# Attention core of a fused two-block kernel: one group of transposes moved ahead of the last score products

## The chip, the cores and the metric

The program runs on one NeuronCore of a Trainium2 chip, in float32 throughout. The metric is the time of one execution on the device in microseconds (us). The core has TensorE (PE in the profile, with its weight loads shown apart as PEld), VectorE (DVE), ScalarE (ACT), GpSimd (POOL) and SyncE (SP, which only issues DMAs here). Each engine works through its own list of instructions in order and waits for the others by semaphores.

## What is computed

Two transformer-like blocks run one after the other in one program. The change touches one part of the first: the attention of 1024 tokens, in 16 heads of 64 values each (8 grouped-query heads on 2 key and value heads, then 8 latent heads with 64 + 32 key dimensions), over 1280 keys, of which 256 come from a context.

```python
def block_attention(q, k, v, scale):
    ...
    def one_block(qi):
        s = jnp.einsum("bqhgd,bkhd->bhgqk", _f32(qi), kf) * scale
        p = jax.nn.softmax(s, axis=-1)
        return jnp.einsum("bhgqk,bkhe->bqhge", p, vf)
...
        o_a = block_attention(q_a, k_a, v_a, GQA_HEAD_DIM ** -0.5)
        o_m = block_attention(q_m, k_m, v_m, (MLA_NOPE_DIM + MLA_ROPE_DIM) ** -0.5)
        o = jnp.concatenate([o_a, o_m], axis=-1)
        return (o * jax.nn.silu(gate)) @ w_out
```

## The kernel before

The attention core is a loop of 64 **stages**. Stage s treats 128 tokens (s // 8) and one pair of heads (p = s % 8, the heads called e = 0 and 1). Pairs 0 to 3 are grouped-query heads, pairs 4 to 7 latent heads. A stage has these steps:

- **Scores** (`scores_pe`, L793 to L819), PE. Each head has its own three PSUM banks, `attn_aux` for e = 0 and `attn_far` for e = 1, for 1280 scores, filled in segments of 512, 512 and 256 keys. A product of L808 uses 64 rows of the array, so the two heads' products lie side by side in it. Latent heads add products over 32 rows for the rotated part: L816 for the first 1024 keys, L819 for the last 256. A float32 product appears as two matmul instructions, each `x1` in the rows. The last segment's products count `scored`.
- **Maximum** (`maximum` in `core_dve`), DVE: for each head one `reduce_max` over its 1280 scores (L915) and a small negation (L917), which counts `negated`.
- **Softmax weights** (`soften` in `core_act`), ACT: for each head one exponential over 1280 scores with the sum accumulated (L896), which counts `exped`. The sum is read out by a short second instruction on the same line.
- **Turn** (`turn_group_pe`, L822 to L839), PE: the weights are transposed in five **groups** j = 0 to 4 of four 128x128 transposes, each group into one of two banks of `attn_dense`: groups 0, 2 and 3 into bank 0, groups 1 and 4 into bank 1. A transpose uses the whole 128x128 array.
- **Copies** out of those banks: groups 0, 1 and 3 by ACT (L885), groups 2 and 4 by DVE (L922). A group waits for the copy that empties its bank (`copied[0]`, `copied[1]`).
- **Weigh** (`weigh_pe`, L843 to L852), PE: 20 products of values and turned weights, 40 instructions on 64 columns of the array, into bank 1; DVE keeps the result (`keep`, L928, counts `stored`). It waits for all copies of its stage, and for this stage's copy 1 and so for bank 1.

The loop is software-pipelined by hand in `core_pe`. In iteration s PE waits for the exponentials of stage s, then does: all scores of stage s + 1, groups 0, 1 and 2 of stage s, the weighing of stage s - 1, groups 3 and 4 of stage s. ACT does copy 0, copy 1, the two exponentials of stage s + 1, copy 3. DVE does a reciprocal (L943), the two maxima of stage s + 1, copy 2, the keep of stage s - 1, copy 4, and once per eight stages a multiplication (L934). So group 3 waits for copy 2, which stands on DVE behind both maxima of the next stage; group 4 waits for the keep, which stands behind copy 2. SP issues DMAs only for the sums, once per eight stages.

After stage 63 comes the rest of the kernel, beginning with the gate projections (L122), which wait for the last keep.

Of the kernel before, what the change touches and what calls it, by code (L numbers as in the profile page):

```python
# [15 lines left out]
L = 1024  # L16
LT = L // P
C = 256
N = L + C
# [5 lines left out]
ROPE = 32  # L25
# [38 lines left out]
def segments(cols):  # L64

    return [(a, min(a + BANK, cols)) for a in range(0, cols, BANK)]
# [88 lines left out]
STAGES = 8 * LT  # L155
# [569 lines left out]
def values_pe(pe, Y, t):  # L725

    if t == 0:
        pe.wait_ge(Y.aux_read, len(Y.use))
    elif t == 2:
        pe.wait_ge(Y.vm_read, 1)  # L730
    elif t == 3:
        pe.wait_ge(Y.vm_read, 2)
    elif t == 4:
        pe.wait_ge(Y.va_read, 2)
    elif EARLY <= t < EARLY + 2:
        pe.wait_ge(Y.dense.emptied[t - EARLY], Y.dense.at["u7"] + 1)
    elif t >= EARLY:
        pe.wait_ge(Y.vm_read, t - 1)
    pe.matmul(values_bank(Y, t), Y.ckv[:, t * P:(t + 1) * P], Y.wv[:], start=True, stop=True).then_inc(Y.vm_filled, 1)
# [47 lines left out]
def stage(s):  # L787

    t, p = divmod(s, 8)
    return slice(t * P, (t + 1) * P), p  # L790


def scores_pe(pe, Y, s):  # L793

    tokens, p = stage(s)
    if s:
        pe.wait_ge(Y.exped, 2 * s)
    else:
        pe.wait_ge(Y.km_read, 4)
        pe.wait_ge(Y.vm_read, EARLY)  # L800
        pe.wait_ge(Y.va_read, len(OWN_GROUPS))
        pe.wait_ge(Y.roped, len(ROPES))
        Y.dense.done(pe, "u3")
    for lo, hi in segments(N):
        for e in range(2):
            rows = slice(64 * e, 64 * e + 64)
            keys = Y.ka[rows, lo:hi] if p < 4 else Y.km[rows, p - 4, lo:hi]
            mm = pe.matmul(Y.scores[e][:, lo:hi], Y.Q[rows, p, tokens], keys, start=True, stop=(p < 4))  # L808
            if p < 4 and hi == N:
                mm.then_inc(Y.scored, 1)  # L810
    if p >= 4:
        for e in range(2):
            for n, (lo, hi) in enumerate(segments(L)):
                first = 64 * e + ROPE * n
                rows = slice(first, first + ROPE)
                pe.matmul(Y.scores[e][:, lo:hi], Y.Q[rows, p + 4, tokens], Y.kpe[rows, lo:hi], start=False, stop=True)  # L816
        for e in range(2):
            rows = slice(64 * e, 64 * e + ROPE)
            pe.matmul(Y.scores[e][:, L:N], Y.Q[rows, p + 4, tokens], Y.kpe[rows, L:N], start=False, stop=True).then_inc(Y.scored, 1)  # L819


def turn_group_pe(pe, Y, s, j):  # L822

    bank = Y.banks[j % 2] if j < 3 else Y.banks[(j + 1) % 2]
    if s == 0 and j < 2:
        pe.wait_ge(Y.vm_read, NT)
    if s or j >= 2:
        if j in (0, 2, 3):
            pe.wait_ge(Y.copied[0], 3 * s + (0, 0, 1, 2)[j])
        elif j == 1:  # L830
            pe.wait_ge(Y.copied[1], 2 * s)
        else:
            pe.wait_ge(Y.copied[1], 2 * s + 1)
            if s:
                pe.wait_ge(Y.stored, s)
    for e in range(2):
        for kk in range(2):
            n, k = 2 * e + kk, 2 * j + kk
            tr = pe.transpose(bank[:, n * P:(n + 1) * P], Y.probs[:, s % 2, e, k * P:(k + 1) * P], Y.ident)  # L839
    tr.then_inc(Y.turned_up, 1)  # L840


def weigh_pe(pe, Y, s):  # L843

    tokens, p = stage(s)
    bank = Y.banks[1]
    pe.wait_ge(Y.copied[1], 2 * (s + 1) + (1 if s + 1 < STAGES else 0))
    pe.wait_ge(Y.copied[0], 3 * (s + 1))
    for k in range(NT):
        for e in range(2):  # L850
            v = Y.va[:, k, 64 * e:64 * e + 64] if p < 4 else Y.vm[:, k, HD * (2 * (p - 4) + e):HD * (2 * (p - 4) + e + 1)]
            mm = pe.matmul(bank[64 * e:64 * e + 64, 0:P], v, Y.turned[:, s % 2, 4 * (k // 2) + 2 * e + k % 2], start=(k == 0),  # L852
                           stop=(k == NT - 1))
    mm.then_inc(Y.weighed, 1)


def core_pe(pe, Y):
    scores_pe(pe, Y, 0)
    for t in range(EARLY, NT):
        values_pe(pe, Y, t)  # L860
    for s in range(STAGES):
        pe.wait_ge(Y.exped, 2 * s + 2)
        if s + 1 < STAGES:
            scores_pe(pe, Y, s + 1)
        for j in range(3):
            turn_group_pe(pe, Y, s, j)
        if s:
            weigh_pe(pe, Y, s - 1)
        for j in (3, 4):
            turn_group_pe(pe, Y, s, j)  # L870
    weigh_pe(pe, Y, STAGES - 1)
# [269 lines left out]
def attention_layer(nc, arena, A, x_out, mod, one_plus, K):  # L1141
    with Phase(nc, "attn") as ph:
        Y = Attention(nc, ph, arena, A, mod, one_plus, K)
        with ph.block() as block:
            @block.sync
            def _(sp):
                attention_sp(sp, Y)
                store_halves(sp, Y, x_out)

            @block.tensor  # L1150
            def _(pe):
                front_pe(pe, Y)
                core_pe(pe, Y)
                back_pe(pe, Y)

            @block.scalar
            def _(act):
                front_act(act, Y, A["x"], A["ctx"])
                core_act(act, Y)
                back_act(act, Y)  # L1160

            @block.vector
            def _(dve):
                front_dve(dve, Y)
                core_dve(dve, Y)
                back_dve(dve, Y)
# [2780 lines left out]
```

## Time and profile before

| | us |
|---|---|
| runs of the kernel (3) | 4828.37, 4829.55, 4832.45; median 4829.55 |
| profiled execution: device time | 4826.16 |
| profiled execution: span, first to last instruction | 4824.4 |
| PE busy | 4628.4 (96%) |
| DVE busy | 2090.0 (43%) |
| ACT busy | 1008.9 (21%) |
| the attention core in the span | from 297.8 to 853.3 |

The busy shares are means over the whole kernel. The attention core is about a ninth of it and repeats itself: between the first and last few stages, an iteration that scores a grouped-query pair looks like every other such iteration, and one that scores a latent pair likewise. What the change does can be read from one iteration of each kind, start by start: the profile gives each instruction's start and duration, and for an idle engine who released it. Ends of matmuls are modelled, so that consecutive ones overlap in the rows; for PE, the distance of starts is what counts. The granted clock was 1.00 in the core except for its first 13 us.

### The profile page before, as it was taken

To read this page: it belongs to the slowest core of one execution; us is meant where nothing else is said; L and a number is where in the kernel's file an instruction comes from. 1 tells how busy PE (TensorE), PEld (TensorE's weight loads), DVE (VectorE), ACT (ScalarE), POOL (GpSimd) and SP (SyncE) were. 2 spreads that over 40 slices of the span, in tenths; PEclk is the share of its full clock that TensorE was granted. 3 is DMA by queue.
4 is the path that set the end of the run, shared out by engine and by line. 5 is a ranking of instruction groups with operands and counts; after the bars stand their busy time and mean duration, and the time that the engine had idled before them with its cause. 6 is when DMAs were issued, how large, how long until landed. Compare 5 with 4: busy or idle time off the path is not lost.

```text
span 4824.4 us, 39417 instructions
## 1 busy us (share of the span) xinstructions
PE 4628.4 (96%) x16488; PEld 2291.1 (47%) x16488; DVE 2090.0 (43%) x2485; ACT 1008.9 (21%) x1349; POOL 3.9 (0%) x7
## 2 busy tenths in 40 slices
PE   7999999999999999999999999999999999999998
PEld 3456666443444444554555554444444444444443
DVE  3555555134333466644344433513643354333412
ACT  3145555111111100002333222322310010000000
POOL 0000000000000000000000000000000000000000
PEclk9999999998999999999999999999999999999999
DMA  6100000222231522221111011012231131111211
GB/s 247 71 27 10 10 10 6 105 78 88 81 105 69 197 101 104 100 97 57 40 35 36 32 35 42 33 44 74 72 107 39 40 109 48 44 44 44 76 44 55
DMA packets 106812, 320.27 MB, mean 66 GB/s; under 512 B 26085, under 2 KB 44261, under 8 KB 99082
## 3 DMA queue, kind: packets, MB, share of 16 engines
q1 hardware_dynamic: 89708, 306.22, 17.9%
q10 hardware_dynamic: 16928, 11.54, 0.7%
q8 instruction: 131, 2.15, 0.2%
q14 instruction: 45, 0.37, 0.0%
HBM read 257.36 MB, written 60.36 MB: 66 GB/s over the span
## 4 chain that ended last, share of the span: by engine, by line
PE 67%; DVE 8%; issue 1%; DMA 1%; ACT 1%; DVEq 0%; SPq 0%; ACTq 0%
PE late_dense L122 31%; PE late_four L3281 10%; PE late_two L3281 5%; PE late_four L3510 3%; PE late_four L1403 3%; PE late_four L2341 2%; PE late_four L1592 2%; PE late_dense L3510 1%; PE late_two L1680 1%; PE late_two L1672 1%; PE late_four L1420 1%; PE late_four L1415 1%; PE late_two L3510 1%; PE late_two L1609 1%; DVE arena L2577 1%
## 5 line engine op out<-in xcount | busy, mean ns | idle before, releaser
L122 PE MATMUL late_dense<-arena 128*128 128x512 f32 x4008 | 1778.0, 601 | 18.5 <-ACT arena L135 7.6
L122 PEld LDWEIGHTS late_dense<-arena 128*128 128x128 f32 x4008 | 765.1, 193 | 960.5 <-issue 951.5
L3281 PE MATMUL late_four<-arena 128*128 128x512 f32 x1160 | 506.5, 594 | 5.9 <-DVE arena L3111 5.9
L135 ACT ACTIVATE arena<-late_dense 128x512 f32<-128x512 f32 x198 | 118.0, 596 | 1162.2 <-PE late_dense L122 1140.6
L3281 PEld LDWEIGHTS late_four<-arena 128*128 128x128 f32 x1160 | 221.1, 191 | 284.7 <-issue 274.9
L122 PE MATMUL attn_dense<-arena 128*128 128x512 f32 x640 | 281.3, 597 | 4.2 <-ACT arena L637 2.1
L3281 PE MATMUL late_two<-arena 128*128 128x512 f32 x576 | 253.4, 592 | 0.0
L3329 DVE TENSOR_TENSOR arena<-late_four,arena 128x512 f32<-128x512 f32 x145 | 98.7, 690 | 300.5 <-PE late_four L3281 296.1
L839 PE MATMUL attn_dense<-matrices,arena 128*128 128x128 f32 x1280 | 187.6, 282 | 18.2 <-ACT arena L885 16.1
L122 PEld LDWEIGHTS attn_dense<-arena 128*128 128x128 f32 x640 | 121.1, 191 | 158.5 <-issue 153.8
L1403 PE MATMUL late_four<-arena 128*128 128x512 f32 x384 | 171.6, 600 | 7.8 <-DMA arena<-in_hy_tables 3.9
L3281 PEld LDWEIGHTS late_two<-arena 128*128 128x128 f32 x576 | 109.4, 190 | 137.8 <-issue 135.8
L839 PEld LDWEIGHTS attn_dense<-matrices,arena 128*128 128x128 f32 x1280 | 135.4, 141 | 72.2 <-issue 32.1
L885 ACT ACTIVATE arena<-attn_dense 128x512 f32<-128x512 f32 x192 | 107.8, 596 | 242.4 <-PE attn_dense L839 234.4
L915 DVE TENSOR_REDUCE arena<-attn_aux 128x1 f32<-128x1280 f32 x64 | 95.5, 1491 | 145.2 <-PE attn_far L819 90.2
L808 PE MATMUL attn_aux<-arena 64*128 64x512 f32 (+1 forms) x384 | 156.0, 540 | 1.6 <-ACT arena L770 0.8
L808 PE MATMUL attn_far<-arena 64*128 64x512 f32 (+1 forms) x384 | 156.1, 540 | 0.0
L852 PE MATMUL attn_dense<-arena 128*64 128x128 f32 x2560 | 153.9, 275 | 0.8 <-DVE arena L922 0.8
L852 PEld LDWEIGHTS attn_dense<-arena 128*64 128x64 f32 x2560 | 138.4, 137 | 11.6 <-ACT arena L885 10.6
L3510 PE MATMUL late_four<-arena 128*128 128x512 f32 x320 | 139.0, 592 | 0.0
L2341 PE MATMUL late_four<-arena 128*128 128x64 f32 (+3 forms) x1024 | 97.7, 283 | 26.5 <-DVE arena L2489 14.3
L1403 PEld LDWEIGHTS late_four<-arena 128*128 128x128 f32 x384 | 72.5, 191 | 100.7 <-issue 93.1
(384 smaller groups left out, 4703.0 us busy)
## 6 DMA issues: line engine op xcount, KB each, us to landing
arena<-in_ada_w SPq DMA_DIRECT2D x12, 2048.0 KB, 8.5
arena<-in_w_ffn_in SPq DMA_DIRECT2D x44, 512.0 KB, 4.0
arena<-in_hy_tables SPq DMA_DIRECT2D x16, 1280.0 KB, 6.1
arena<-in_hy_w_in SPq DMA_DIRECT2D x32, 512.0 KB, 3.3
spectrum<-arena SPq DMA_DIRECT2D x8, 2048.0 KB, 8.8
arena<-spectrum SPq DMA_DIRECT2D x8, 2048.0 KB, 12.7
arena<-in_w_gates SPq DMA_DIRECT2D x32, 512.0 KB, 3.3
spill<-arena SPq DMA_DIRECT2D x26, 512.0 KB, 4.4
```

The lines of the kernel that those rows point to most:

```text
L122: mm = pe.matmul(self.ps[:, n % SEG], self.wbuf[:, slot, k], job.rhs[:, k, cols], start=(job.first and k == 0), stop=(job.last and k == kt ...
L135: act.activation(job.out[:, cols], self.ps[:, n % SEG], job.func, scale=job.scale, bias=job.bias).then_inc(self.emptied[n % SEG], 1)
L808: mm = pe.matmul(Y.scores[e][:, lo:hi], Y.Q[rows, p, tokens], keys, start=True, stop=(p < 4))
L839: tr = pe.transpose(bank[:, n * P:(n + 1) * P], Y.probs[:, s % 2, e, k * P:(k + 1) * P], Y.ident)
L852: mm = pe.matmul(bank[64 * e:64 * e + 64, 0:P], v, Y.turned[:, s % 2, 4 * (k // 2) + 2 * e + k % 2], start=(k == 0), stop=(k == NT - 1))
L885: act.activation(dst, src, ACT.Copy).then_inc(sem, 1)
L1403: mm = pe.matmul(Y.group[:, 2 * a + part], Y.table[:, r, part, k], rhs[:, 2 * r + k], start=(k == 0), stop=(k == 1))
L1592: mm = pe.matmul(group[:, 2 * (q % 2) + way], Y.hid[:, q * P:(q + 1) * P], Y.mix[:, way, cols], start=True, stop=True)
L2341: mm = pe.matmul(ps[:, (u + h) % 2, queries], left[t.rows[h], at], right[t.rows[h], queries], start=True, stop=True)
L3281: mm = pe.matmul(product_bank(M, name, i), left[:, k], right[:, k], start=(k == 0), stop=(k == 3))
L3329: dve.tensor_tensor(out, product_bank(M, product, i), other, ALU.add).then_inc(M.summed_up, 1)
L3510: mm = pe.matmul(bank, left[:, k], right[:, k], start=(first and k == 0), stop=(last and k == count - 1), skip_group_check=True)
```

## The change

The score products of the last 256 keys leave `scores_pe` for a function of their own, `last_scores_pe`. In iteration s PE now does: the scores of stage s + 1 but for that last piece, group 0 of stage s, the last piece of the scores, groups 1 and 2, and then the weighing and groups 3 and 4 as before. For a grouped-query pair the last piece is L808's segment of 256 keys (2 products, 4 instructions); for a latent pair it is L819's (also 2 products, 4 instructions), while L808's three segments stay ahead. Every instruction stays, with its operands and its semaphores; nothing changes on ACT, DVE, POOL or SP.

```diff
-    for lo, hi in segments(N):
-        for e in range(2):
-            rows = slice(64 * e, 64 * e + 64)
-            keys = Y.ka[rows, lo:hi] if p < 4 else Y.km[rows, p - 4, lo:hi]
-            mm = pe.matmul(Y.scores[e][:, lo:hi], Y.Q[rows, p, tokens], keys, start=True, stop=(p < 4))
-            if p < 4 and hi == N:
-                mm.then_inc(Y.scored, 1)
+    for lo, hi in segments(N)[0:2 if p < 4 else 3]:
+        head_scores_pe(pe, Y, s, lo, hi)
     if p >= 4:
...
-        for e in range(2):
-            rows = slice(64 * e, 64 * e + ROPE)
-            pe.matmul(Y.scores[e][:, L:N], Y.Q[rows, p + 4, tokens], Y.kpe[rows, L:N], start=False, stop=True).then_inc(Y.scored, 1)
+
+
+def head_scores_pe(pe, Y, s, lo, hi):
+
+    tokens, p = stage(s)
+    for e in range(2):
+        rows = slice(64 * e, 64 * e + 64)
+        keys = Y.ka[rows, lo:hi] if p < 4 else Y.km[rows, p - 4, lo:hi]
+        mm = pe.matmul(Y.scores[e][:, lo:hi], Y.Q[rows, p, tokens], keys, start=True, stop=(p < 4))
+        if p < 4 and hi == N:
+            mm.then_inc(Y.scored, 1)
+
+
+def last_scores_pe(pe, Y, s):
+
+    tokens, p = stage(s)
+    if p < 4:
+        head_scores_pe(pe, Y, s, L, N)
+        return
+    for e in range(2):
+        rows = slice(64 * e, 64 * e + ROPE)
+        pe.matmul(Y.scores[e][:, L:N], Y.Q[rows, p + 4, tokens], Y.kpe[rows, L:N], start=False, stop=True).then_inc(Y.scored, 1)
...
 def core_pe(pe, Y):
     scores_pe(pe, Y, 0)
+    last_scores_pe(pe, Y, 0)
...
         if s + 1 < STAGES:
             scores_pe(pe, Y, s + 1)
-        for j in range(3):
+        turn_group_pe(pe, Y, s, 0)
+        if s + 1 < STAGES:
+            last_scores_pe(pe, Y, s + 1)
+        for j in (1, 2):
             turn_group_pe(pe, Y, s, j)
```

## Rows read from the trace of the kernel before

**Rows 1.** The page's first line: the span of the profiled execution.

```profile
span 4824.4 us, 39417 instructions
```

**Rows 2.** Stretches: us, busy of PE, PEld, DVE, ACT, POOL, PEclk, DMA, GB/s.

```profile
307.90:311.20 3.30, 3.29 (x8) 1.62 (x10) 0.07 (x1) 0.35 (x1) 0.00 (x0) 0.50 0.00 0
311.20:319.00 7.80, 5.54 (x38) 3.41 (x34) 4.56 (x7) 4.41 (x7) 0.00 (x0) 1.00 0.00 0
450.00:850.00 400.00, 387.62 (x3696) 269.58 (x3692) 233.47 (x383) 211.99 (x330) 0.00 (x0) 1.00 0.05 9
```

**Rows 3.** Timeline, PE, one iteration scoring a grouped-query pair: start us, us, instruction.

```profile
580.37 0.69 PE L808 MATMUL attn_aux<-arena 64*128 64x512 f32 x1
580.90 0.59 PE L808 MATMUL attn_aux<-arena 64*128 64x512 f32 x1
...
582.19 0.38 PE L808 MATMUL attn_aux<-arena 64*128 64x256 f32 x1
...
582.41 0.38 PE L808 MATMUL attn_aux<-arena 64*128 64x256 f32 x1
...
582.72 1.09 PE L839 MATMUL attn_dense<-matrices,arena 128*128 128x128 f32 x8
584.06 0.66 PE L839 MATMUL attn_dense<-matrices,arena 128*128 128x128 f32 x4 [0.25 <-ACT arena L885]
584.65 2.40 PE L852 MATMUL attn_dense<-arena 128*64 128x128 f32 x40
```

**Rows 4.** Timeline, PE, in narrow windows around its changes of work there.

```profile
582.89 0.49 PE L839 MATMUL attn_dense<-matrices,arena 128*128 128x128 f32 x3
...
584.45 0.27 PE L839 MATMUL attn_dense<-matrices,arena 128*128 128x128 f32 x1
...
586.78 0.28 PE L852 MATMUL attn_dense<-arena 128*64 128x128 f32 x2
586.99 0.33 PE L839 MATMUL attn_dense<-matrices,arena 128*128 128x128 f32 x1
...
587.90 0.27 PE L839 MATMUL attn_dense<-matrices,arena 128*128 128x128 f32 x1
588.10 0.69 PE L808 MATMUL attn_aux<-arena 64*128 64x512 f32 x1
```

**Rows 5.** Timeline, DVE, same iteration.

```profile
582.82 1.49 DVE L915 TENSOR_REDUCE arena<-attn_aux 128x1 f32<-128x1280 f32 x1 [1.58 <-PE attn_far L808]
...
586.00 0.68 DVE L922 COPY arena<-attn_dense 128x512 f32<-128x512 f32 x1
587.11 0.29 DVE L928 COPY arena<-attn_dense 128x128 f32<-128x128 f32 x1 [0.42 <-PE attn_dense L852]
```

**Rows 6.** Timeline, ACT, same iteration: copies 0 and 1, and the second exponential's read-out.

```profile
583.41 0.60 ACT L885 ACTIVATE arena<-attn_dense 128x512 f32<-128x512 f32 x1 [2.86 <-PE attn_dense L839]
583.91 0.59 ACT L885 ACTIVATE arena<-attn_dense 128x512 f32<-128x512 f32 x1
...
587.35 0.19 ACT L896 ACTIVATION_READ_ACCUMULATOR arena<-attn_far,arena 128x1 f32 x1
```

**Rows 7.** Timeline, PE and DVE, one iteration scoring a latent pair, and the next's start.

```profile
631.21 0.69 PE L808 MATMUL attn_aux<-arena 64*128 64x512 f32 x1
...
635.15 1.49 DVE L915 TENSOR_REDUCE arena<-attn_aux 128x1 f32<-128x1280 f32 x1 [3.07 <-PE attn_far L819]
...
640.43 0.69 PE L808 MATMUL attn_aux<-arena 64*128 64x512 f32 x1
```

**Rows 8.** Timeline, the first iteration's group 3, and the turn of iterations 62 and 63.

```profile
315.90 1.09 PE L839 MATMUL attn_dense<-matrices,arena 128*128 128x128 f32 x8 [2.01 <-DVE arena L922]
...
843.06 0.19 ACT L896 ACTIVATION_READ_ACCUMULATOR arena<-attn_far,arena 128x1 f32 x1
843.40 0.60 ACT L885 ACTIVATE arena<-attn_dense 128x512 f32<-128x512 f32 x1
```

**Rows 9.** Waits from 319 to 840 us: total us, times, longest.

```profile
PE attn_dense L839 <- ACT arena L885: 15.6, 62, 0.3
```

## Prediction

> **What bounds the kernel now.** I read first where the change acts: the attention core, 297.8 to 853.3 us of a span of 4824.4 us [rows 1]. The stretches show PE busy for 387.62 of 400 us there, DVE and ACT for little more than half, clock 1.00 [rows 2]. Then I took the timeline of one iteration, engine by engine. From one first score product to the next it lasts 588.10 - 580.37 = 7.73 us where a grouped-query pair is scored [rows 3, 4], and 640.43 - 631.21 = 9.22 us where a latent pair is [rows 7]. PE sets this length, with one real gap: the eight transposes of groups 0 and 1 last start at 582.72 + 1.09 - 0.27 = 583.54, and group 2 starts at 584.06, 0.05 us after copy 0 ends (583.41 + 0.60) [rows 3, 4, 6]. That is 0.41 us more than the usual step of 0.11 from transpose to transpose ((0.49 - 0.27)/2) [rows 4], and the waits list it 62 times [rows 9]. It is the gap that the move closes: with score products between groups 0 and 1, copy 0 is over before group 2 is due.
>
> The second thing to read is how late the other chain runs, from the last score product through DVE: both maxima, copy 2, group 3. From the start of the first maximum to that of copy 2 are 586.00 - 582.82 = 3.18 us, copy 2 takes 0.68 [rows 5]; I add 0.05 for the handover to PE, as at copy 0. Were group 3 to start there, then groups 3 and 4 take 0.82 from first to last start (as groups 0 and 1: 1.09 - 0.27) and the next scores start 0.20 later (587.90 to 588.10) [rows 3, 4]. Sum: 3.18 + 0.68 + 0.05 + 0.82 + 0.20 = 4.93 us from maximum to next iteration. Now the maximum starts at 2.45 us into the iteration (582.82 - 580.37), or at 3.94 in a latent one (635.15 - 631.21) [rows 3, 5, 7]. 2.45 + 4.93 = 7.38 against 7.73, and 3.94 + 4.93 = 8.87 against 9.22: this chain has a **slack of 0.35 us** in either kind.
>
> **The change, part by part.** Nothing is removed or added; three things move.
>
> *Group 0 earlier.* Its copy is off ACT's hands before copy 1 is wanted. Gains the 0.41 us at group 2 and no more; what comes next is worked out below.
>
> *The last score products later.* The maximum waits for them. They now stand behind four transposes: 4 x 0.11 = 0.44 us [rows 4]. No row of before has score products between transposes, so the two additional changes of work are priced by the rows of such changes elsewhere. Into transposes: from the last products at 582.41 to 582.72 are 0.31 us, where two products of 256 keys are 582.41 - 582.19 = 0.22 apart, so 0.09 extra, and the first transpose takes 0.17 (582.72 to 582.89) instead of 0.11, another 0.06: 0.15 [rows 3, 4]. Into products: 587.90 to 588.10 is 0.20 instead of 0.11, and the first product takes 0.53 (580.37 to 580.90) instead of 0.43 (a third of 580.90 to 582.19): 0.19 [rows 3, 4]. Together 0.34 us an iteration. The bounds: nothing at all from below (a transpose after a transpose pays nothing, though it waits on a semaphore), and twice this from above; changes from and to the weighing cost the same 0.09 (584.45 to 584.65, and 586.78 to 586.99, against 0.11) [rows 3, 4], so I take 0.34.
>
> The Trainium skill, "TensorEngine Tiling (Array Packing)", section Key Properties, says that a change of tiling mode drains TensorE. The rows agree: 64-row products, full transposes and 64-column weighing each cost some 0.09 us to enter. A reader who counted instructions alone would find no cost in this move; by that page each interleaving costs two drains, which speaks against the change, and without them my sum would be that of the cheap case below.
>
> *The maximum, and all behind it.* It starts 0.44 + 0.34 = **0.78 us later**; the slack is 0.35. Queued behind it on DVE are copy 2 and the keep, and on ACT the exponentials and copy 3; PE's group 3 waits for copy 2. In the grouped-query iteration: maximum at 3.23, copy 2 ends at 3.23 + 3.18 + 0.68 = 7.09, group 3 at 7.14, next scores at 3.23 + 4.93 = 8.16 us. Not later than that: the weighing waits for copy 1, which starts now 583.91 - 583.54 = 0.37 after the last transpose of group 1 (0.31 when ACT is free: 583.41 less group 0's last start, 582.89 + 0.22), so at 3.17 + 0.34 + 0.31 = 3.82, ends at 4.41, and the weighing starts at 4.46 and would let group 3 go at 4.46 + (586.99 - 584.65 = 2.34) = 6.80, before 7.14 [rows 3, 4, 6]. The keep ends at 7.09 + 0.29 = 7.38, before group 4 is due at 7.14 + 0.17 + 3 x 0.11 = 7.64 [rows 5]. The exponentials end 587.35 + 0.19 - 582.82 = 4.72 after the maximum starts, before 4.93 [rows 5, 6].
>
> So the length is 8.16 instead of 7.73, in latent iterations 3.94 + 0.78 + 4.93 = 9.65 instead of 9.22: **0.43 us more** each. The gap at group 2 is gone, and a wait of 0.34 us at group 3 (7.14 against 6.80) and one at the weighing stand in its place.
>
> *The sum.* 63 iterations score a next stage. The first has no slack: its group 3 already waited 2.01 us for copy 2 [rows 8], so it pays 0.78. In the last of them copy 3 bounds what follows; it started at 843.40, and the exponentials ended at 843.06 + 0.19 = 843.25 [rows 8]: slack 0.15, so 0.63. The other 61 pay 0.43: 26.2. In all 26.2 + 0.78 + 0.63 = 27.6 us. Nothing after the core gives it back: the gate projections start when the last keep is done, and their loads were issued long before or wait for the same end. SP's DMAs of the sums and the multiplication L934 come once in eight stages; DVE has more free time per iteration than now, so they cost nothing; without that cover L934 would cost its length, eight times.
>
> The profiled execution would go from 4826.16 to 4853.8 us. The median of the runs is 3.39 us above that execution, so I forecast 4829.55 + 27.6 = **4857.2 us**.
>
> **The rivals.**
>
> *Changes of work are cheap* (0.10). If the two additional ones cost nothing, the maximum is only 0.44 late and the iteration 0.44 - 0.35 = 0.09 longer: 61 x 0.09 + 0.44 + 0.29 = 6.2 us, 4835.8 us. For it: between groups 0 and 1 there is no extra cost. Against it: each of the four changes of shape in these rows costs 0.09 or 0.10 on entry [rows 3, 4].
>
> *Faster, by the closed gap* (0.05). If the maximum came no later than the slack allows, PE's own order would decide. Copy 1 would start 0.31 after group 1 instead of 0.37, end at 584.44, and the weighing would start at 584.49 instead of 584.65: 0.16 less, 61 times, 9.8 us, 4819.8 us [rows 3, 4, 6]. It decides from a delay of the maximum under 0.35 - 0.16 = 0.19 us, and any gain ends at 0.35; the four transposes alone take 0.44. Only if the transposes slipped in beside the products would it happen.
>
> *Changes of work are dear* (0.08). At twice the price the maximum is 1.12 late: 61 x 0.77 + 1.12 + 0.97 = 49 us, 4878.6 us. For it: the order products, transposes, products has no row.
>
> *The clock falls* (0.03). PE is idle twice in an iteration instead of once. At clock 0.50 work takes double [rows 2]; PE works for some 7.3 us in an iteration (7.73 less the gap), so one iteration in ten at that clock would add 6 x 7.3 = 44 us to mine, about 4901 us. Against it: a gap of 2.01 us in the first iteration left the clock at 1.00 [rows 2, 8], and the new ones are under 0.5. The Trainium skill, "TensorE: Matmul & The Clock Gate", section "A second HAM failure mode: psum-queue depth-cycling", says that frequent small gaps between groups of matmuls can make the clock go back and forth; the rows of before, with a gap in every iteration at 1.00, don't show it.
>
> **How the numbers follow.** Forecast 0.74, and the rivals as given. The range goes from the cheap case, 4835, to 4872, where a change of work costs 1.7 times mine (1.02 late: 61 x 0.67 + 1.02 + 0.87 = 42.8 us); it leaves out the faster case, the falling clock and most of the dear one, some 0.16. A measurement of this kernel can tell about 0.2% from no change, here 9.7 us: 4819.9 to 4839.2. The cheap case lies within. Faster 0.05, the same 0.11, slower 0.84.
>
> **What would show it.** In the changed kernel's timeline: iterations of 8.16 and 9.65 us; group 3 right behind copy 2, so that the waits have TensorE's L839 on DVE's L922 some 60 times, and no longer L839 on ACT's L885; the keep starting with no idle time before it; copy 0 and copy 1 apart on ACT; the last score products 0.20 after group 0's last transpose. It would be wrong if the maximum started less than 0.35 us later in the iteration, if group 3 did not wait, or if the rest after the core ran shorter or longer than before.

## The result

The changed kernel takes 4861.91 us (median of 4 runs, 4858.84 to 4863.14), the kernel before 4828.96 us on the same chip (4 runs). The ratio is 1.0067, with a 95% interval from 1.0053 to 1.0080: **slower by 33 us**. The forecast was 28 us slower, 4857.2 us. The profiled execution took 4861.71 us, its span is 4859.9 us. A second measurement of the same program on another chip gave 4863.11 against 4831.26 us, ratio 1.0067 (1.0044 to 1.0090).

Two stretches of each trace, from the first score products to the gate projections and from there to the end, say where the time went (columns as in [rows 2]; x counts instructions). Kernel before:

```profile
297.79:853.35 555.56, 533.12 (x5003) 367.76 (x5003) 318.59 (x519) 292.97 (x454) 0.00 (x0) 1.00 0.04 8
853.35:4824.40 3971.05, 3826.19 (x10620) 1795.51 (x10620) 1627.22 (x1871) 637.96 (x798) 3.69 (x3) 0.97 0.20 69
```

Changed kernel, its page's first line and the same two stretches, with the middle of the core (450 to 850 us):

```profile
span 4859.9 us, 39417 instructions
...
295.99:882.08 586.09, 546.12 (x5002) 363.38 (x5003) 312.76 (x519) 293.10 (x454) 0.00 (x0) 0.99 0.04 8
882.08:4859.90 3977.82, 3833.23 (x10620) 1798.52 (x10620) 1627.29 (x1871) 638.31 (x798) 3.69 (x3) 0.97 0.20 69
...
450.00:850.00 400.00, 376.60 (x3488) 252.11 (x3486) 219.81 (x367) 202.33 (x316) 0.00 (x0) 1.00 0.05 9
```

The core is 586.09 - 555.56 = 30.5 us longer. The part behind it, whose code is the same, is 6.8 us longer in this execution; the part ahead of the core is 1.8 us shorter. More on that below.

One iteration that scores a grouped-query pair, timeline of PE in the changed kernel; it answers to [rows 3, 4]. L820 was L808, L853 was L839, L866 was L852:

```profile
603.10 0.69 PE L820 MATMUL attn_aux<-arena 64*128 64x512 f32 x1
...
604.49 0.59 PE L820 MATMUL attn_aux<-arena 64*128 64x512 f32 x1
...
605.02 0.65 PE L853 MATMUL attn_dense<-matrices,arena 128*128 128x128 f32 x4
605.60 0.48 PE L820 MATMUL attn_aux<-arena 64*128 64x256 f32 x1
...
605.92 0.38 PE L820 MATMUL attn_aux<-arena 64*128 64x256 f32 x1
...
606.23 1.09 PE L853 MATMUL attn_dense<-matrices,arena 128*128 128x128 f32 x8
...
607.58 2.40 PE L866 MATMUL attn_dense<-arena 128*64 128x128 f32 x40 [0.25 <-ACT arena L903]
...
610.25 1.09 PE L853 MATMUL attn_dense<-matrices,arena 128*128 128x128 f32 x8 [0.27 <-DVE arena L940]
...
611.27 0.69 PE L820 MATMUL attn_aux<-arena 64*128 64x512 f32 x1
```

Its DVE and ACT, which answer to [rows 5, 6]:

```profile
606.33 1.49 DVE L933 TENSOR_REDUCE arena<-attn_aux 128x1 f32<-128x1280 f32 x1 [2.37 <-PE attn_far L820]
606.93 0.60 ACT L903 ACTIVATE arena<-attn_dense 128x512 f32<-128x512 f32 x1 [0.63 <-PE attn_dense L853]
...
609.52 0.68 DVE L940 COPY arena<-attn_dense 128x512 f32<-128x512 f32 x1
...
610.11 0.28 DVE L946 COPY arena<-attn_dense 128x128 f32<-128x128 f32 x1
```

The gap at group 2 is closed: groups 1 and 2 are one row of eight transposes at 606.23. The maximum starts 606.33 - 603.10 = 3.23 us into the iteration instead of 2.45. Copy 2 ends at 610.20, group 3 starts 0.05 after it, the keep follows copy 2 with no idle time, and the next scores start after 8.17 us instead of 7.73. A latent iteration lasts 629.13 - 619.45 = 9.68 us instead of 9.22:

```profile
619.45 0.69 PE L820 MATMUL attn_aux<-arena 64*128 64x512 f32 x1
...
629.13 0.69 PE L820 MATMUL attn_aux<-arena 64*128 64x512 f32 x1
```

In the waits of the core (319 to 870 us), TensorE's wait for ACT at L839 [rows 9] has gone, and two others stand there, on copy 2 and on copy 1:

```profile
PE attn_dense L853 <- DVE arena L940: 16.5, 61, 0.3
PE attn_dense L866 <- ACT arena L903: 15.5, 62, 0.3
```

### The profile page after: what moved, and what is told of

It reads as the page before. It is cut to its first block, busy times and chain, and to the rows that moved or that the text cites. A ratio compares the mean times of both kernels' runs of the same rounds, so it can differ in the third digit from the quotient of the medians.

```text
span 4859.9 us, 39417 instructions
## 1 busy us (share of the span) xinstructions
PE 4646.6 (96%) x16488; PEld 2287.7 (47%) x16488; DVE 2084.3 (43%) x2485; ACT 1009.4 (21%) x1349; POOL 3.9 (0%) x7
## 3 DMA queue, kind: packets, MB, share of 16 engines
q8 instruction: 131, 2.15, 0.2%
## 4 chain that ended last, share of the span: by engine, by line
PE 67%; DVE 7%; issue 1%; DMA 1%; ACT 1%; DVEq 0%; SPq 0%; ACTq 0%
PE late_dense L122 31%; PE late_four L3299 10%; PE late_two L3299 5%; PE late_four L3528 3%; PE late_four L1421 3%; PE late_four L2359 2%; PE late_four L1610 2%; PE late_dense L3528 1%; PE late_two L1698 1%; PE late_two L1690 1%; PE late_four L1438 1%; PE late_four L1433 1%; PE late_two L3528 1%; PE late_two L1627 1%; DVE arena L2595 1%
## 5 line engine op out<-in xcount | busy, mean ns | idle before, releaser
L3299 PEld LDWEIGHTS late_four<-arena 128*128 128x128 f32 x1160 | 221.3, 191 | 285.2 <-issue 275.4
L853 PE MATMUL attn_dense<-matrices,arena 128*128 128x128 f32 x1280 | 182.0, 281 | 20.2 <-DVE arena L940 19.7
L853 PEld LDWEIGHTS attn_dense<-matrices,arena 128*128 128x128 f32 x1280 | 136.5, 141 | 105.8 <-issue 69.9
L866 PE MATMUL attn_dense<-arena 128*64 128x128 f32 x2560 | 153.9, 275 | 16.3 <-ACT arena L903 15.5
L820 PE MATMUL attn_aux<-arena 64*128 64x512 f32 (+1 forms) x384 | 165.6, 552 | 1.6 <-ACT arena L770 0.8
L820 PE MATMUL attn_far<-arena 64*128 64x512 f32 (+1 forms) x384 | 165.7, 552 | 0.0
L866 PEld LDWEIGHTS attn_dense<-arena 128*64 128x64 f32 x2560 | 138.4, 137 | 31.4 <-ACT arena L903 30.4
L2359 PEld LDWEIGHTS late_four<-arena 128*128 128x128 f32 (+1 forms) x1024 | 98.7, 205 | 50.3 <-issue 32.8
```

The source lines that it names most:

```text
L2359: mm = pe.matmul(ps[:, (u + h) % 2, queries], left[t.rows[h], at], right[t.rows[h], queries], start=True, stop=True)
L3299: mm = pe.matmul(product_bank(M, name, i), left[:, k], right[:, k], start=(k == 0), stop=(k == 3))
```

## The experiments

The theory: the loss is the delay of the maximum beyond its slack of 0.35 us, carried by copy 2 to group 3. The main rival: the loss is PE's own, from the two additional changes of work. Times of one experiment are beside runs of the kernel before on its own chip.

### The delay without the move

```diff
 dve.wait_ge(Y.scored, 2 * s + e + 1)
+if s and e == 0:
+    dve.reduce_max(Y.select[:, 0:1], Y.ka[:, 0:690], AX_X)
 dve.reduce_max(Y.top[:, at:at + 1], Y.scores[e][:, 0:N], AX_X).then_inc(Y.topped, 1)
```

> The kernel before, PE's order untouched, with one idle maximum over 690 elements put on DVE between the wait for the scores and the first maximum of each stage, so that the maximum starts about 0.78 us later (0.72 to 0.9). Theory (the delay of the maximum beyond 0.35 us is the whole loss): 8.16 and 9.65 us (8.1 to 8.3), with the gap at group 2 still there: about 28 us slower than before, 4857 us (4852 to 4864), nearly what the change costs. Rival (PE's additional changes of work carry a good part of the loss): clearly less, 0.1 us an iteration, 6 us.

Measured: 4858.61 us against 4828.39, ratio 1.0063 (1.0046 to 1.0079). PE's order is that of before. Timeline of PE and DVE in one iteration:

```profile
602.48 0.69 PE L808 MATMUL attn_aux<-arena 64*128 64x512 f32 x1
...
604.93 0.87 DVE L916 TENSOR_REDUCE arena<-arena 128x1 f32<-128x690 f32 x1 [1.58 <-PE attn_far L808]
...
605.72 1.48 DVE L917 TENSOR_REDUCE arena<-attn_aux 128x1 f32<-128x1280 f32 x1
...
609.63 1.10 PE L839 MATMUL attn_dense<-matrices,arena 128*128 128x128 f32 x8 [0.46 <-DVE arena L924]
...
610.65 0.69 PE L808 MATMUL attn_aux<-arena 64*128 64x512 f32 x1
```

The maximum is 605.72 - 604.93 = 0.79 us late, and the iteration lasts 8.17 us: the length of the changed kernel, with no transposes moved. The gap at group 2 is still open: from 319 to 870 us TensorE waits for ACT at L839 62 times, 15.6 us in all, as before. The delay is enough for the whole loss of an iteration.

### A delay below the slack

The same added line, over 230 elements instead of 690.

> The kernel before with an idle maximum over 230 elements on DVE ahead of each stage's first maximum, the 690-element one of the run before cut to a third: that one delayed the maxima by 0.79 us, this one should by 0.79 - 460 x 1.04 ns = 0.31 us. Theory (0.35 us of slack): iterations of 7.73 and 9.22 us, as the kernel before, nothing lost. Rival (no slack; each delay counts in full or in part): 0.1 to 0.3 us an iteration, 8 to 19 us in all.

Measured: 4828.88 us against 4831.26, ratio 0.9996 (0.9984 to 1.0007).

```profile
594.91 0.69 PE L808 MATMUL attn_aux<-arena 64*128 64x512 f32 x1
...
597.37 0.39 DVE L916 TENSOR_REDUCE arena<-arena 128x1 f32<-128x230 f32 x1 [1.58 <-PE attn_far L808]
597.67 1.48 DVE L917 TENSOR_REDUCE arena<-attn_aux 128x1 f32<-128x1280 f32 x1
...
602.64 0.69 PE L808 MATMUL attn_aux<-arena 64*128 64x512 f32 x1
```

The maximum is 0.30 us late and the iteration still lasts 7.73 us. The slack is real: a delay of 0.30 loses nothing, one of 0.79 loses 0.44, and 0.79 - 0.44 = 0.35.

### The move without the delay

The maxima over fewer scores, in the changed order and, as a control, in the old one. They leave out the last 256 scores (L is 1024, N is 1280), but still wait for all of them. Both kernels also scale the exponent by 0.001, so their softmax is another one; they serve for timing alone.

```diff
-dve.reduce_max(Y.top[:, at:at + 1], Y.scores[e][:, 0:N], AX_X).then_inc(Y.topped, 1)
+dve.reduce_max(Y.top[:, at:at + 1], Y.scores[e][:, 0:L], AX_X).then_inc(Y.topped, 1)
```

> The kernel before with the same shortened maxima and the same scale of the exponent. Control: its chain through DVE has slack already, so both theories expect 7.73 and 9.22 us and no change of the whole time, 4829 us. If DVE were the bound of the kernel before, it would be up to 0.53 us an iteration faster.

> The changed kernel's order on PE, with the maxima taken over the first 1024 of the 1280 scores (and the exponent's scale set to 0.001, so that nothing overflows; the result is another softmax). Each maximum is some 0.27 us shorter, which gives the chain through DVE 0.53 us. Theory: PE alone is then the bound, the weighing waits for copy 1 and starts at 4.48 us, and from there to the next scores are 3.45 us as before: 7.93 and 9.43 us, still 0.20 us longer than the same shortening in the old order, about 13 us on the whole. Rival (the move is a gain by itself, and only the maximum spoils it): 7.57 and 9.06 us, 10 us less than the old order.

Measured against 4828.39 us: the old order 4827.64 us, ratio 0.9998 (0.9987 to 1.0008); the new order 4841.46 us, ratio 1.0026 (1.0014 to 1.0038). New order, PE and DVE:

```profile
602.01 0.69 PE L820 MATMUL attn_aux<-arena 64*128 64x512 f32 x1
...
605.25 1.23 DVE L933 TENSOR_REDUCE arena<-attn_aux 128x1 f32<-128x1024 f32 x1 [2.37 <-PE attn_far L820]
...
606.50 2.40 PE L866 MATMUL attn_dense<-arena 128*64 128x128 f32 x40 [0.25 <-ACT arena L903]
...
609.94 0.69 PE L820 MATMUL attn_aux<-arena 64*128 64x512 f32 x1
```

The iteration lasts 7.93 us: with the maxima out of the way the move still costs 0.20 us, and 13.8 us in all (4841.46 - 4827.64). The weighing starts 4.49 us into the iteration, behind copy 1, where it started at 4.28 before. The gap of 0.41 us is closed, but the wait for copy 1 takes most of that back: of the 0.35 us for the changes of work only some 0.15 are recovered (the prediction's faster rival had 0.16). So the hope that only the maximum spoils the move falls. In the old order shorter maxima bring nothing: DVE is no bound there.

### Copy 2 off the chain

```diff
 copy(s, 0)
 copy(s, 1)
+copy(s, 2)
 if s + 1 < STAGES:
     soften(s + 1)
```

in `core_act` of the changed kernel, and `copy(s, 2)` taken out of `core_dve`.

> The changed kernel with one thing more: copy 2 of each stage is done by ACT, right after copy 1, instead of by DVE behind both maxima. Theory (the late maximum holds group 3 through copy 2): group 3 no longer waits for DVE; what is late next are the exponentials, which end 4.72 us after the maximum starts, so the next scores start at 3.23 + 4.72 + 0.05 = 8.0 us: iterations of 8.0 and 9.5 us instead of 8.18 and 9.68, about 10 us less than the changed kernel, 4851 us. Rival (the two additional changes of work on PE are the cost, DVE only follows): iterations stay at 8.18 and 9.68 us, 4862 us.

Measured: 4848.82 us against 4828.39, ratio 1.0042 (1.0026 to 1.0058), 13 us below the changed kernel's 4861.91, on other chips. PE, DVE and ACT:

```profile
600.39 0.66 PE L820 MATMUL attn_aux<-arena 64*128 64x512 f32 x1
...
603.63 1.49 DVE L934 TENSOR_REDUCE arena<-attn_aux 128x1 f32<-128x1280 f32 x1 [2.54 <-PE attn_far L820]
...
608.16 0.19 ACT L914 ACTIVATION_READ_ACCUMULATOR arena<-attn_far,arena 128x1 f32 x1
...
608.49 0.66 PE L820 MATMUL attn_aux<-arena 64*128 64x512 f32 x1
```

The direction is right and group 3 waits for DVE no more, but the iteration lasts 8.10 us, not 8.0. The exponentials end at 608.35, 4.72 us after the maximum starts, as expected; the scores that wait for them start 0.14 us later, not 0.05. I had used the handover of copy 0 to transposes; this one goes from ACT's read-out to score products. Of the 13 us, the 60 iterations from the third on give 4.8 (0.08 each); the core is 581.2 us long against 586.1, and in the profiled executions the rest lies mostly behind the core, where the code is the same (3969.0 us against 3977.8). So the whole time confirms the direction only; the copy's worth is the 0.08 us of the iteration.

### Half of a group ahead

```diff
-turn_group_pe(pe, Y, s, 0)
+turn_group_pe(pe, Y, s, 0, (0,))
 if s + 1 < STAGES:
     last_scores_pe(pe, Y, s + 1)
+turn_group_pe(pe, Y, s, 0, (1,))
```

The last argument names the heads whose two transposes are issued; the semaphore comes with head 1.

> The changed kernel with half as much ahead of the last score products: only the two transposes of head 0 of group 0, the two of head 1 behind them. Theory (the delay of the maximum, 0.22 + 0.34 = 0.56 us, less the slack of 0.35): 7.94 and 9.43 us, 14 us slower than before, 4843 us. Rival (each interleaving costs its changes of work, whatever lies between): 8.18 and 9.68 us, as the changed kernel.

Measured: 4854.42 us against 4827.0, ratio 1.0056 (1.0033 to 1.0079): neither of the two expectations, but between them. PE, DVE and ACT:

```profile
601.52 0.69 PE L820 MATMUL attn_aux<-arena 64*128 64x512 f32 x1
...
604.54 1.49 DVE L935 TENSOR_REDUCE arena<-attn_aux 128x1 f32<-128x1280 f32 x1 [2.15 <-PE attn_far L820]
604.92 1.08 ACT L905 ACTIVATE arena<-attn_dense 128x512 f32<-128x512 f32 x2 [3.21 <-PE attn_dense L853]
605.57 0.66 PE L853 MATMUL attn_dense<-matrices,arena 128*128 128x128 f32 x4 [0.25 <-ACT arena L905]
...
609.60 0.69 PE L820 MATMUL attn_aux<-arena 64*128 64x512 f32 x1
```

The iteration lasts 8.08 us, not 7.94. The chain through the maximum behaves as the theory says: the maximum is at 3.02, and 3.02 + 4.93 = 7.95. But I had overlooked PE's own order. Group 0 is complete only behind the last score products, so its copy ends no sooner relative to group 1 than before, and the gap at group 2 is back. PE then pays the two changes of work in full: 7.73 + 0.35 = 8.08. This run shows PE's price by itself: with the gap open again, nothing of it is given back, where the short maxima, with the gap closed, left 0.20.

### Two groups ahead

Groups 0 and 1 ahead of the last score products, group 2 behind.

> The changed kernel with twice as much ahead of the last score products: groups 0 and 1. Theory: the maximum is another 0.44 us late, 1.22 in all, so 8.61 and 10.11 us, 27 us slower than the changed kernel, 4889 us. Rival (changes of work alone count): 8.18 and 9.68 us.

Measured: 4885.8 us (2 runs) against 4827.0, ratio 1.0123 (1.0093 to 1.0152).

```profile
608.52 0.69 PE L820 MATMUL attn_aux<-arena 64*128 64x512 f32 x1
...
612.19 1.49 DVE L933 TENSOR_REDUCE arena<-attn_aux 128x1 f32<-128x1280 f32 x1 [2.80 <-PE attn_far L820]
...
616.11 1.09 PE L853 MATMUL attn_dense<-matrices,arena 128*128 128x128 f32 x8 [1.03 <-DVE arena L940]
...
617.13 0.69 PE L820 MATMUL attn_aux<-arena 64*128 64x512 f32 x1
```

The maximum is at 3.67 us, 0.44 later than in the changed kernel, and the iteration lasts 8.61 us, 0.44 longer: beyond the slack a delay counts in full.

### Half of the iterations

```diff
+late = s + 1 < STAGES and stage(s + 1)[1] < 4
+if s + 1 < STAGES and not late:
+    last_scores_pe(pe, Y, s + 1)
 turn_group_pe(pe, Y, s, 0)
-if s + 1 < STAGES:
+if late:
     last_scores_pe(pe, Y, s + 1)
```

> The change in the 31 iterations that score a grouped-query pair alone; those that score a latent pair keep the old order. Theory: iterations don't lean on each other, so the 31 last 8.18 us and the 32 others 9.22 us: some 14.5 us slower than before, 4843 us. Rival (a late iteration's debt is paid back or grows in the next): the latent iterations behind a grouped-query one differ from 9.22 us.

Measured: 4841.89 us against 4827.0, ratio 1.0028 (1.0014 to 1.0041).

```profile
606.02 0.69 PE L820 MATMUL attn_aux<-arena 64*128 64x512 f32 x1
...
614.20 0.69 PE L820 MATMUL attn_aux<-arena 64*128 64x512 f32 x1
...
623.43 0.69 PE L820 MATMUL attn_aux<-arena 64*128 64x512 f32 x1
```

8.18 us for the grouped-query iteration, and 9.23 for the latent one right behind it, as in the kernel before (9.22). An iteration's loss isn't paid back or added to in the next, and half of them cost 15 us of the 33.

### The changed kernel again

> The changed kernel once more, word for word, for a second trace. Theory: the core takes the same time as in the first trace, 586.1 us from its first score products to the gate projections, with the third iteration again 1.7 us longer than the others of its kind, since the gap that the change lengthens in the first iteration lets the clock fall; what lies behind the core differs by several us either way, by where the clock falls there. Rival: the part behind the core is again some 7 us longer than in the kernel before, so that the change costs something there too.

The core took 584.87 us, 1.2 us less than in the first trace, and what lies behind it 3977.90 us, as long as in the first:

```profile
883.40:4861.30 3977.90, 3833.54 (x10620) 1797.80 (x10620) 1627.86 (x1871) 638.20 (x798) 3.69 (x3) 0.97 0.20 69
```

What the expectation calls the third iteration is the second of the loop; it lasts 9.67 us, again too long, and the granted clock was again 0.50 there, from 316.6 to 320.0 us. The first iteration lasts 8.33 us here and 9.55 in the first trace. In this trace the clock was at 1.00 in all but its last 0.4 us, in the first trace it was at 0.50 for the first 2.8 us. That is the 1.2 us between the two cores.

For the part behind the core, the rival's expectation is what came: 3977.8 and 3977.9 us against 3971.05. But the traces don't sort by the change. With the last scores moved in any way it took 3977.8 us (half a group), 3974.9 (short maxima), 3974.2 (two groups), 3972.3 (half of the iterations) and 3969.0 (copy 2 on ACT), and with the old order 3974.3 (short maxima), 3974.0 (small delay) and 3972.0 (delay alone, whose core is as long as the changed one's). The code there is the same in all of them. What goes along with it is for how long the clock was granted at half: behind the core, the records add up to 252 and 249 us in the two traces of the changed kernel, to 231 before, and to 228 in the shortest of all, that of copy 2 on ACT. Whether the change has a part in this is left open; there is one trace of the kernel before.

## Why the prediction was right

**The bound and its slack: right.** Iterations of 8.17 and 9.68 us stand against the forecast 8.16 and 9.65, group 3 starts at 7.15 us against 7.14. The chain of 4.93 us from maximum to scores is 611.27 - 606.33 = 4.94. The slack of 0.35 was tested from both sides, at 0.30 and 0.79.

**The changes of work: right in size.** No row of before had products between transposes. Entering group 0 takes 605.02 - 604.49 = 0.53 instead of 0.43, 0.10 more. The other three transposes of group 0 are this row:

```profile
605.18 0.49 PE L853 MATMUL attn_dense<-matrices,arena 128*128 128x128 f32 x3
```

The last one starts at 605.18 + 0.49 - 0.27 = 605.40. So entering the last products takes 605.60 - 605.40 = 0.20 instead of 0.11, and the first of them 605.92 - 605.60 = 0.32 instead of 0.22. The maximum is 3.23 - 2.45 = 0.78 late, the forecast to the hundredth; in the latent iteration it is 0.81 late (it starts 4.75 us in, not 3.94), which is where 9.68 instead of 9.65 comes from. The half group paid 0.35 of PE's time where I had 0.34. The Trainium skill says that a change of tiling mode drains TensorE ("TensorEngine Tiling (Array Packing)", Key Properties). The rows agree in that both new boundaries cost extra time; what the array does in that time they don't show. The cheap case would have needed the maximum 0.44 late, the dear one 1.12.

**The wait that takes the gap's place: right.** Both waits are there, 61 and 62 times. The weighing starts at 607.58 - 603.10 = 4.48 (forecast 4.46), behind copy 1.

**The sum: right, with small terms off.** The 60 iterations from the third on cost 0.45 to 0.46 each, 27.3 us; I had 0.43. The first cost 0.53 instead of 0.78: it lasts 315.67 - 306.12 = 9.55 us against 9.02 (307.91 to 316.93). This term isn't like for like, since both run in part at half clock, for 3.3 us before and 2.8 here. The last cost 0.54 instead of 0.63. And the second lasts 9.88 us instead of 8.17, because 3.4 us of it were at a granted clock of 0.50:

```profile
314.65 1.09 PE L853 MATMUL attn_dense<-matrices,arena 128*128 128x128 f32 x8 [2.92 <-DVE arena L940]
...
315.80:319.20 3.40, 3.40 (x8) 1.02 (x8) 0.74 (x2) 0.14 (x1) 0.00 (x0) 0.50 0.00 0
```

The first row is group 3 in the first iteration, from the timeline, the second a stretch behind it, as in [rows 2]. 27.3 + 0.53 + (9.88 - 7.73 = 2.15) + 0.54 = 30.5 us, the measured difference of the cores. With the second trace it is 584.87 - 555.56 = 29.3 us.

**The clock: the step that failed.** I wrote that the gap of 2.01 us in the first iteration left the clock at 1.00 and that the new gaps are under 0.5. I missed that this very gap is the one that the delay lengthens, to 2.92 us (2.93 in the second trace), and that the clock falls behind it. It happens once and costs 1.7 us (the second iteration against the forecast 8.17; 1.5 in the second trace), not the 44 of the rival that I had priced. That the longer gap is the cause fits these traces and isn't shown: the last section has the other runs' gaps. In the other iterations, with two gaps each, the granted clock stayed at 1.00, as the stretch from 450 to 850 us shows; the going back and forth of which the Trainium skill speaks ("TensorE: Matmul & The Clock Gate", "A second HAM failure mode: psum-queue depth-cycling") did not come.

**The rest after the core: the sign of being wrong that did come.** The prediction put nothing on the part behind the core, and named a longer one as a sign that it was wrong. It was 6.8 and 6.9 us longer in the two traces of the changed kernel. The forecast of the core doesn't rest on it, but the prediction had no term for how much this part differs from one execution to the next: 3969.0 to 3977.9 us over all the traces here.

**What is left.** 33 us against 28. Of the medians' 33 us the core has 30.5 or 29.3, by the trace; 2.5 to 3.7 us are left. In the first profiled pair 35.5 - 30.5 = 5.0 us lie outside the core. Their cause stays open, as above. The mechanism gives most of the 33: 27.3 us in the 60 iterations alone. How well the rest of the sum came out was not in the prediction's hands: the part behind the core differs by up to 9 us between traces, and the part ahead of it by 3 (295.6 to 298.5 us).

## What to carry to other kernels

A gap on the busiest engine is worth only what the next chain leaves of it. Before work is moved into a gap, take the length of the loop and subtract every chain that passes through the moved work, here 2.45 + 4.93 against 7.73; the difference is all the delay that the move may cause. Count also what the filler costs on entry and exit, and which wait comes next once the gap is closed: here two changes between score products and transposes cost 0.35 us, the closed gap of 0.41 gave back only some 0.15, because the weighing then waited for copy 1, and so even without the other chain 0.20 us were lost.

## What the runs showed of the hardware

The length of one gap does not say whether the clock falls. These are the waits of TensorE at group 3 of the first iteration, and whether the granted clock fell to 0.50 in the next few microseconds. It fell behind 2.92 and 2.93 us (the two traces of the changed kernel), 2.79 (delay alone), 2.92 (half of the iterations), 3.37 (two groups) and 2.24 (half a group). It stayed at 1.00 behind 1.46 (short maxima, old order), 2.01 (before), 2.29 (small delay) and 2.39 us (short maxima, new order). With copy 2 on ACT it fell after two waits, of 0.74 and 2.04 us. So 2.24 was enough once and 2.39 was not.

A handover has no single price either: from a copy on DVE to transposes it took 0.05 us (610.20 to 610.25), from a copy on ACT to the weighing 0.05 (607.53 to 607.58), from the read-out of an exponential's sum on ACT to score products 0.14 (608.35 to 608.49, in the run with copy 2 on ACT).

Transposes put between 64-row score products cost TensorE 0.34 us beyond their own 0.11 each in the changed kernel (0.78 - 0.44), and 0.35 in the run with half a group ahead (8.08 - 7.73).
